# Norm transitions of a hybrid encoder: transpositions in two parts, another order of low parts, nine constant products

## What is computed

```python
for i in range(2):
    sh1, sc1, g1, sh2, sc2, g2 = split(silu(c) @ ada_w[i] + ada_b[i], 6)
    h = rmsnorm(x, norm_w[i, 0]) * (1 + sc1) + sh1
    h = gated_deltanet(h, ...) if i == 0 else conformer_conv(h, ...)
    x = x + (1 + g1) * rmsnorm(h, norm_w[i, 1])
    h = rmsnorm(x, norm_w[i, 2]) * (1 + sc2) + sh2
    h = (silu(h @ W_gate) * (h @ W_up)) @ W_out
    x = x + (1 + g2) * rmsnorm(h, norm_w[i, 3])

def conformer_conv(h):                  # layer 1
    a, gate = split(h @ pw1_w + pw1_b, 2)
    u = depthwise_conv(a * sigmoid(gate), dw_w) + dw_b      # width 31
    return silu(layernorm(u)) @ pw2_w + pw2_b
```

## Time and profile before

| | us |
|---|---|
| median of 3 runs | 3030.74 (3026.4 to 3035.09) |
| the profiled execution | 3030.81 |
| its span, first to last instruction | 3029.2 |
| TensorE busy in it | 2828.1 |
| VectorE busy | 2201.4 |
| ScalarE busy | 1273.3 |

### The profile page before, as it was taken

The page is one execution under the profiler, slowest core; times in us unless marked ns, Lnnn a source line. Parts: engine busy times, 40 slices in busy tenths (PEclk is TensorE's granted clock), DMA queues, the critical chain, the costliest instruction groups (busy, mean ns, idle before and its releaser), DMA issues.

```text
span 3029.2 us, 38342 instructions
## 1 busy us (share of the span) xinstructions
PE 2828.1 (93%) x14064; PEld 2236.0 (74%) x14064; DVE 2201.4 (73%) x2255; ACT 1273.3 (42%) x1447; POOL 181.2 (6%) x327
## 2 busy tenths in 40 slices
PE   1699999998889989999999998999889999999998
PEld 1577888876765868888888886444768888888886
DVE  7599989886882868888888885299756655555565
ACT  2356744336983454333333334201345333333333
POOL 0012211132231000000000000000000000000000
PEclk8799999999999999999999998999999999999998
DMA  9777787667654959888898983544256666656663
GB/s 399 286 252 274 280 301 255 203 208 222 207 166 170 376 197 356 334 302 339 326 344 334 347 334 117 167 152 153 70 179 251 203 201 206 208 202 214 207 205 114
DMA packets 322176, 731.65 MB, mean 242 GB/s; under 512 B 48128, under 2 KB 64336, under 8 KB 293648
## 3 DMA queue, kind: packets, MB, share of 16 engines
q1 hardware_dynamic: 316256, 709.85, 66.4%
q0 software_dynamic: 5808, 20.35, 1.9%
HBM read 710.45 MB, written 19.69 MB: 241 GB/s over the span
## 4 chain that ended last, share of the span: by engine, by line
PE 81%; DVE 9%; ACT 4%; DMA 3%; issue 2%; DVEq 0%; SPq 0%; ACTq 0%
PE psg L733 44%; PE psg L739 22%; PE psg L720 7%; DMA aring<-in_ada_w 2%; DVE wlo L1181 2%; PE pst L710 1%; PE psn L1034 1%; DVE cv L1424 1%; PE psn L1144 1%; DVE y L1725 1%; ACT rv L2109 1%; DVE aacc L1299 1%; PE psn L760 1%; DMA wraw<-d_rr 0%; PE psn L710 0%
## 5 line engine op out<-in xcount | busy, mean ns | idle before, releaser
L1849 ACT ACTIVATE whi<-wraw 128x2048 fp32r<-128x2048 f32 x400 | 766.4, 1916 | 1180.7 <-PE psg L739 1057.1
L1181 DVE TENSOR_TENSOR wlo<-wraw,whi 128x2048 fp32r<-128x2048 f32 x400 | 916.6, 2292 | 456.0 <-ACT whi L1849 455.4
L733 PE MATMUL psg<-whi,h_hi 128*128 128x512 f32 x2304 | 725.2, 396 | 23.1 <-DVE h_lo L1805 13.2
L733 PE MATMUL psg<-whi,h_lo 128*128 128x512 f32 x2304 | 714.6, 391 | 0.0
L739 PE MATMUL psg<-wlo,h_hi 128*128 128x512 f32 x2304 | 572.3, 391 | 7.9 <-DVE wlo L1181 7.9
L733 PEld LDWEIGHTS psg<-whi,h_hi 128*128 128x128 f32 x2304 | 431.4, 189 | 115.3 <-issue 25.7
L739 PEld LDWEIGHTS psg<-wlo,h_hi 128*128 128x128 f32 x2304 | 433.8, 188 | 99.4 <-DVE wlo L1181 9.3
L733 PEld LDWEIGHTS psg<-whi,h_lo 128*128 128x128 f32 x2304 | 436.0, 189 | 92.3
L1191 DVE SCALAR_TENSOR_TENSOR aacc<-aring,cond,aacc 128x2048 f32<-128x2048 f32 x150 | 351.9, 2346 | 6.2 <-DMA aring<-in_ada_w 5.8
L720 PE MATMUL psg<-wraw,aring 128*128 128x512 f32 x512 | 221.1, 592 | 0.0
L733 PE MATMUL psg<-whi,g_hi 128*128 128x512 f32 x704 | 219.5, 393 | 0.0
(11 more groups left out here) (316 smaller groups left out, 2336.8 us busy)
## 6 DMA issues: line engine op xcount, KB each, us to landing
aring<-in_ada_w SPq DMA_DIRECT2D x192, 1024.0 KB, 7.4
wraw<-in_ffn_in_w SPq DMA_DIRECT2D x176, 1024.0 KB, 6.9
wraw<-in_gdn_in_w SPq DMA_DIRECT2D x96, 1024.0 KB, 5.3
wraw<-in_ffn_out_w SPq DMA_DIRECT2D x88, 1024.0 KB, 5.2
wraw<-in_cf_pw_w SPq DMA_DIRECT2D x48, 1024.0 KB, 5.3
wraw<-in_gdn_out_w SPq DMA_DIRECT2D x32, 1024.0 KB, 8.7
rr_even<-d_rr SPq DMA_DIRECT2D x8, 1024.0 KB, 6.6
wraw<-d_rr SPq DMA_DIRECT2D x8, 1024.0 KB, 5.7
```

The lines of the kernel that those rows point to most:

```text
L733: mm(ps[:, t, 0:width], a[:, kc, t * P:(t + 1) * P], wh, start=first and j + n == 0, stop=False)
L1181: tt(wlo[:, j % 2, :], wraw[:, j % 4, :], whi[:, j % 2, :].bitcast(F32), SUB).then_inc(w_lo, 1)
L1849: av(whi[:, j % 2, :], wraw[:, j % 4, :], ACT.Copy).then_inc(w_hi, 1)
```

## The change

- Before the transpositions of each `pre` and before pw2, TensorE does nine products of constants (identity by 512 columns of the norm weights) into PSUM that nobody reads.
- `pre`: quarters 0 and 1 are transposed in two halves, the first 128 tokens as soon as their half of y is there. Quarters 2 and 3 are transposed behind the first weight tile in both FFNs (for pw1 directly).
- ScalarE makes the high part of quarter 0 before it modulates quarter 1; VectorE makes low part 0 before the weight low part of tile 1. `hi` and `lo` of tile 2 of an FFN are moved into `pre`, ahead of the quarters 2 and 3 (on VectorE between low parts 2 and 3).
- Last column of the DeltaNet's projection: no copy; ScalarE squares and VectorE multiplies it straight from PSUM, half by half.
- Layer norm: the low parts lie between the passes over the quarters.

The parts of the diff stand in this order: TensorE; VectorE (`pre`, first FFN's entry, FFN, layer norm); ScalarE.

```diff
+            def constants():
+                for _ in range(9):
+                    mm(pst[:, 0:2, :].rearrange("p a t -> p (a t)"), ident[:, :], vec[:, 0:NSL], start=True, stop=True)
             def pre(n, src):
-                for q in range(4):
-                    if q == 0:
-                        pe.wait_ge(xn_ok, TT * (n + 1))
-                    if q >= 2:
-                        pe.wait_ge((hf_v, hf_s)[q % 2], 2 * n + 1)
-                    ps = (pst, psn)[q % 2]
+                constants()
+                for t in range(TT):
+                    pe.wait_ge(xn_ok, TT * n + t + 1)
+                    for q in range(2):
+                        for j in range(4):
+                            i = tr((pst, psn)[q][:, j, t * P:(t + 1) * P], src[:, t, (4 * q + j) * P:(4 * q + j + 1) * P])
+                        if t == TT - 1:
+                            i.then_inc(pre_tr, 1)
+                if n == 2:
+                    pre_rest(n, src)
+            def pre_rest(n, src):
+                for q in range(2, 4):
+                    pe.wait_ge((hf_v, hf_s)[q % 2], 2 * n + 1)
                     for j in range(4):
                         for t in range(TT):
-                            i = tr(ps[:, j, t * P:(t + 1) * P], src[:, t, (4 * q + j) * P:(4 * q + j + 1) * P])
+                            i = tr((pst, psn)[q % 2][:, j, t * P:(t + 1) * P], src[:, t, (4 * q + j) * P:(4 * q + j + 1) * P])
                     i.then_inc(pre_tr, 1)
...
-                sl(s0, (0, 0), g0, whole, h_hi3, h_lo3, ready=lambda j: (pre_lo, 4 * n_pre + j + 1))
+                sl(s0, (0, 0), g0, whole, h_hi3, h_lo3, ready=lambda j: (pre_lo, 4 * n_pre + j + 1),
+                   after=lambda j: pre_rest(n_pre, y) if j == 0 else None)
...
             square_sums(3)
+            constants()
...
-                    if q == 0 and weights:
-                        weights()
-                    low(q // 2)
+                    if q == 0:
+                        low(0)
+                        weights(1)
+                        low(1)
                 low(2)
+                weights(2)
                 low(3)
...
+            def out_last(t):
+                dve.wait_ge(yq_ok, 7 + t)
+                i = tt(yg[:, t, 3 * NSL:4 * NSL], psg[:, (S_GO + 3) % 2, t, :], cwb0[:, 3 * NSL:4 * NSL], MUL)
...
                 for j in range(8):
-                    if j >= 2:
+                    if j >= 3:
                         lo(g0 + j, g0 + j)
...
-            for q in range(1, 4):
+
+            def scaled(q):
                 center(q)
                 lv.wait(dve)
                 scale(q)
...
+            scaled(1)
             low(0)
+            scaled(2)
+            low(1)
             lo(G_P2 + 1, G_P2 + 1)
-            for q in range(1, 4):
-                low(q)
+            scaled(3)
+            low(2)
+            low(3)
...
-                odd(1)
                 high(0)
+                odd(1)
                 high(1)
+                weights()
                 high(2)
                 odd(3)
                 high(3)
...
-            y_evac(3)
-            out_squares(0, 3, yg, dump0[:, :], (ps_read, S_F0))
+            act.wait_ge(w_used, G_GO + 32)
+            for t in range(TT):
+                act.wait_ge(yq_ok, 6 + t)
+                av(dump0[:, :], psg[:, (S_GO + 3) % 2, t, :], ACT.Square, accum_out=spart[:, t, 3:4]).then_inc(yq_ok, 1)
```

More of the change, by code:

```diff
@@ L1263, in post_col @@
                 tt(yj, yj, cw[:, j * NSL:(j + 1) * NSL].unsqueeze(1).broadcast_to([P, TT, NSL]), MUL).then_inc(yc_ok, 1)
+            def out_last(t):
+                dve.wait_ge(yq_ok, 7 + t)
+                i = tt(yg[:, t, 3 * NSL:4 * NSL], psg[:, (S_GO + 3) % 2, t, :], cwb0[:, 3 * NSL:4 * NSL], MUL)
+                if t == TT - 1:
+                    i.then_inc(ps_read, 1)
             def post(n, yb, cw):
@@ L1269, in post @@
                 nc.vector.tensor_reduce(r, spart[:, :, :], axis=AX, op=ADD).then_inc(yr_ok, 1)
-                post_col(n, 3, yb, cw)
+                if n:
+                    post_col(n, 3, yb, cw)
+                else:
+                    out_last(1)
                 dve.wait_ge(yrt_ok, n + 1)
@@ L1273, in post @@
                 dve.wait_ge(yr_ok, 2 * n + 2)
-                dve.wait_ge(yc_ok, 4 * (n + 1))
+                dve.wait_ge(*((yc_ok, 4 * n + 3) if n else (ps_read, S_F0)))
                 for t in range(TT):
@@ L1617, in _ @@
             dve.wait_ge(x_land, 32)
+            out_last(0)
             post(0, yg, cwb0)
-            pre(1, y, h_hi3, h_lo3, hf3, 5, 4, lambda: lo(G_F0 + 1, G_F0 + 1))
+            pre(1, y, h_hi3, h_lo3, hf3, 5, 4, lambda j: lo(G_F0 + j, G_F0 + j))
             def ffn(f, g0, s0):
@@ L1832, in _ @@
             post(2, y, cwb)
-            pre(3, y, h_hi3, h_lo3, hf3, 11, 12, lambda: lo(G_F1 + 1, G_F1 + 1))
+            pre(3, y, h_hi3, h_lo3, hf3, 11, 12, lambda j: lo(G_F1 + j, G_F1 + j))
             ffn(1, G_F1, S_F1)
@@ L1877, in root_table, with pre @@
                 av(epsr[:, 3:4], epsr[:, 2:3], ACT.Sqrt)
-            def pre(n, hi_, hfb, low0):
+            def pre(n, hi_, hfb, low0, weights=None):
                 act.wait_ge(aff_ok, n + 1)
@@ L2166, in _ @@
             squares(1, lambda t: (x_up, t + 1))
-            pre(1, h_hi3, hf3, 4)
+            pre(1, h_hi3, hf3, 4, lambda: hi(G_F0 + 2, G_F0 + 2))
             def ffn(f, g0, s0):
@@ L2283, in _ @@
             squares(3, lambda t: (x_up, 5 + t))
-            pre(3, h_hi3, hf3, 12)
+            pre(3, h_hi3, hf3, 12, lambda: hi(G_F1 + 2, G_F1 + 2))
             ffn(1, G_F1, S_F1)
```

## The result

The changed kernel takes 3040.9 us (median of 12 runs, 3036.7 to 3043.9), the kernel before 3032.1 us (12 runs, 3026.4 to 3035.1): the ratio is 1.0024, with a 95% interval from 1.0016 to 1.0032. It is slower by some 7 us (interval 5 to 10). The forecast of +4.8 us had the sign and two thirds of the size; the median of 3040.9 lies just inside the upper end of the range (3041), and the difference is under the 0.3% that were set for a clear one.

What follows compares the result with a forecast made beforehand. TensorE was taken as the bound, with gains only where it stands still. First FFN +3.1, second +4.7, pw1 -1.5, layer norm -1.5 make +4.8 us on 3030.8: forecast 3035.6 us, range 3023 to 3041.

Steps and rivals of the forecast that it cites:

- the mechanism and its place: In both FFNs a late X delays the third ada slice: 3.0 us of TensorE standstill inside tile 3.
- X: In each FFN, the end of the first ada product: forecast at T0 + 15.4 us, before at T0 + 8.65.
- T0: First product of an FFN's first tile: forecast 4.6 us earlier in the first FFN, 3.05 us in the second.
- the clock over tile 0: In both FFNs, half clock over 3 us of tile 0 after a 4.0 us standstill: 1.4 us lost each.
- the fall behind the standstill in tile 3: In both FFNs, half clock after the 3.0 us standstill in tile 3: 1.4 us lost each.
- pw1: Entry of pw1: ScalarE gets quarter 1 sooner, 2.2 us gained at full clock; taken as -1.5 us, bounds -2.2 and 0.
- the layer norm: Layer norm into pw2: 2.9 us gained, 1.4 possibly lost to a clock fall; taken as -1.5, bounds -2.9 and -1.5.
- The constants: Nine constant products at four places: 7.7 us at full clock in TensorE's idle time, delaying nothing, holding the clock meanwhile.
- (1): Rival: the clock is held everywhere, -2.85 us in all, 3027.9 us; chance 0.20.
- (2): Rival: the clock is held and the FFNs' ada slice does not end last, -9.25 us, 3021.5 us; chance 0.12.
- (3): Rival: the fourth ada slice is late too, 2.1 us per FFN, the fifth likewise in one; 3040 to 3042; chance 0.12.
- (4): Rival: constants start at half clock and run into y's first half, +4 us at three entries, 3047 us; chance 0.03.

Runs made afterwards that it cites:

- early ada products: The changed kernel with ada products 0 and 1 of each FFN moved ahead of the late transpositions, right after low part 1: 3031.4 us, 0.9998 of the kernel before.

## Why the prediction was right, and where not

**Right: the mechanism and its place.** X moved behind tile 0, the third ada slice was issued late, and tile 3 stood still: 3.13 and 2.88 us against 3.0 forecast, VectorE's wait 2.60 and 2.33 against 2.4. The run with the early ada products removes it and with it the loss (42.8 and 43.9 us to the gates, 42.8 and 43.0 before). T0 moved by -4.3 us in the first FFN (forecast -4.6) and by 20.96 to 18.58, -2.4 us, in the second (forecast -3.05, or -2.65 with the last transpositions at half clock; the four that modulation waits for took 1.12 us, which is half clock).

**Right, and under-sized: the clock over tile 0.** The step was a half clock over 3 us for 1.4 us of loss, taken from one standstill of 2.8 us. These rows themselves give 3.4 us (means of 0.69 and 0.61 put the half clock from 143.4 to 146.8), so the loss by them was 1.7 us, which the prediction had as its upper bound. It lasted 4.9 and 6.0 us. Tile 0 to tile 1's start without the transpositions took 1134.69 - 1126.85 = 7.8 us and 8.4 us instead of 5.4: 2.4 and 3.0 us. That such a length was possible stood in the trace of the kernel before: behind 3.98 us of products of a single column TensorE ran a weight tile at half clock for 6.1 us (the clock over 570 to 577 is 0.51).

```profile
566.92 3.98 PE L760 MATMUL psn<-ones,aacc 128*128 128x1 f32 x32
...
570.76 1.20 PE L733 MATMUL psg<-whi,h_hi 128*128 128x512 f32 x2
...
576.88 0.62 PE L733 MATMUL psg<-whi,h_lo 128*128 128x512 f32 x2
```

Why it lasts 3 us in one place and 6 in another, no run isolates.

**Half right: the fall behind the standstill in tile 3.** Taken at 1.4 us in both FFNs; it came in the first (1156 to 1159) and not in the second (1.00 at 2310). In the sum of the second FFN this miss cancels the one above, by luck: forecast +4.7, measured +5.45. In the first: forecast +3.1, measured +3.8 to the gate and +4.8 to the end of the FFN. The last 1.0 us is less than executions differ by: from the gate to the end of the FFN, where TensorE has the same instructions in all kernels, the profiled executions took 714.4 to 717.6 us.

**Not settled: pw1.** Forecast -1.5, with bounds of -2.2 and 0; the one profile of the changed kernel has +2.0 to the end of the layer norm's sums, beyond the bound. At its entry nothing was gained: ScalarE's quarter came 1.7 us sooner, and the 16 late transpositions at half clock took as much more. The other 2.0 us are the longer half clock in the convolution (6.9 us for 3.4). In six of the eight other executions with the changed pw1 entry the way in took 17.7 us, 1.7 us less than before and near the forecast, and in all eight the way from the first FFN's end to the end of the sums is 1.5 to 3.2 us shorter than before. So the loss of 2.0 us belongs to one execution and is not a cost of the change. The bounds left out that the clock can fall at another place of a stage that no edit touches.

**Right in most executions: the layer norm.** Tile 0 and the release by ScalarE came as costed (-3.9 us; the third tile waited 1.88 us, forecast 2.3). The fall that was charged at 1.4 us did not come in the changed kernel's profile, which gained 3.0 us for the forecast 1.5. It came in four of the six kernels with this order and the nine constants, which gain 1.4 us. The wait is 1.9 us in all six, and in the second FFN one of 2.88 us passed without a fall, so the length of the standstill alone does not say whether the clock falls.

**Small terms.** The low part of tile 3 was put at T0 + 19.8 before; three tiles of 5.44 us and 16 products of 0.227 make 19.95, so the forecast standstill is nearer to 2.8 us than to 3.0. The prediction's last number, +4.8 us, is the sum of two entries that came out some 0.7 us dearer each to the gates and two stages that no single profile fixes. The interval of the ratio starts at the forecast and ends at twice it, so the mechanism is confirmed by the traces and the experiments, and not by the closeness of the total; that the median still lies inside the range, by 0.1 us, is luck as well.

**The constants** cost nothing and brought nothing that the runs can tell in the changed kernel, as costed.

**The rivals.** (1) and (2) fell: the standstill is in both traces, and the clock was not held. (3), the fourth slice late as well, did not come; VectorE stood 0.62 and 0.64 us before the fourth product (1154.85 and 2311.17), and tile 4 had no wait. (4) fell: the constants ran at full clock at all four places. The profiled execution's span lies 12.1 us over the one before, and 3.9 of it arose before any changed instruction; only the ratio of the many runs, +7 us, is to be held against the forecast.

## What to carry to other kernels

Before work is moved ahead on an engine, list what stands behind it in that engine's order, down to the instruction that frees a buffer: here the reordered norm work pushed the end of a cheap product that nobody waited for back by 4.8 and 7.3 us, and through its buffer and a transfer of some 5 us a weight tile was late. An idle stretch that warms or fills TensorE is a resource; what was taken out of it here (16 transpositions) was paid once in the stream and once more in the clock. Constant products were worth their place here only when they reached up to the next real work, and small gains of this kind are read from the stages of a trace before they can be read from whole runs.

## What the runs showed of the hardware

- The clock at the same place differs between executions of the same instructions. Pw1 and the convolution, with the same standstills (1.11 and 1.99 us) in it, had no half clock (270.3 us), 3.4 us of it (271.7) or 6.9 us (273.7). A profile of one execution thus has steps of 1.7 us in stages that no edit touched.
- A standstill of 1.9 us in a tile stream was followed by half clock in four of six kernels and by none in two; one of 2.88 us was not followed by it, one of 3.13 us was.
- How long half clock lasts behind a standstill does not follow its length: 2.9 us behind 13.15 us (layer norm, kernel before), 4.4 us behind 9.29 (layer norm's order alone), 4.9 and 6.0 us behind 3.78 and 3.95 (changed kernel), 3.2 us behind 3.78 (early ada products, second FFN).
- Behind plain fp32 products of constants the clock was still at 1.00 for 4.1 us and at 0.50 when TensorE began again after 4.90 us; with 0.77 us of standstill behind them tile 0 was at 1.00.
